# A 128-byte buffer in front of `hT` in a decoder trunk: the held operands of TensorE move off their multiples of 512 bytes

## The reference, cut to what matters

```python
def swiglu(h, w_gate, w_up, w_down):
    return (jax.nn.silu(h @ w_gate) * (h @ w_up)) @ w_down
...
for layer in range(DEPTH):
    h = rms_norm(x, mix_norm[layer])
    x = x + hybrid_mixer(h, w_in[layer], ...)
    h = rms_norm(x, ffn_norm[layer])
    if layer % 2 == 0:
        x = x + swiglu(h, dense_w_gate[i], dense_w_up[i], dense_w_down[i])
    else:
        x = x + moe_ffn(h, router_w[i], moe_w_gate[i], moe_w_up[i], moe_w_down[i])
return rms_norm(x, final_norm)
```

## Time and profile before

| | |
|---|---|
| median of 3 runs | 1428.15 us (1425.51 to 1428.62) |
| the profiled execution's own time | 1425.18 us |
| its span, first to last instruction | 1423.6 us |
| granted TensorE clock | 0.998 |
| TensorE matmuls, weight loads | 6506 each |
| HBM traffic over the span | 313 GB/s |

### The profile page before, as it was taken

The page is one execution under the profiler, slowest core; times in us unless marked ns, Lnnn a source line. Parts: engine busy times, 40 slices in busy tenths (PEclk is TensorE's granted clock), DMA queues, the critical chain, the costliest instruction groups (busy, mean ns, idle before and its releaser), DMA issues.

```text
span 1423.6 us, 18360 instructions
## 1 busy us (share of the span) xinstructions
PE 1409.4 (99%) x6506; PEld 1168.6 (82%) x6506; DVE 1174.7 (83%) x1068; ACT 986.9 (69%) x876; POOL 207.9 (15%) x249
## 2 busy tenths in 40 slices
PE   9999999999999999999999999999999999999997
PEld 7888888888888888888888888888888888888885
DVE  6987544548987998889899898888989989888896
ACT  7765444347765877867877777786787777778674
POOL 6840000005831001001001001000100100100010
PEclk9999999999999999999999999999999999999999
DMA  9656555545548899999999999999999999999990
GB/s 359 222 169 215 178 181 198 183 162 196 175 164 310 283 386 378 371 370 409 375 382 372 390 367 371 388 370 369 412 372 384 370 391 366 371 389 373 366 411 33
DMA packets 197552, 445.96 MB, mean 313 GB/s; under 512 B 8400, under 2 KB 19968, under 8 KB 197504
## 3 DMA queue, kind: packets, MB, share of 16 engines
q1 hardware_dynamic: 192496, 432.57, 80.4%
q0 software_dynamic: 2304, 8.39, 2.2%
q10 hardware_dynamic: 2704, 4.38, 0.9%
HBM read 437.97 MB, written 7.34 MB: 313 GB/s over the span
## 4 chain that ended last, share of the span: by engine, by line
issue 58%; PE 34%; POOL 4%; DVE 2%; ACT 1%; DMA 0%; POOLq 0%; ACTq 0%; DVEq 0%
PE bank L1467 10%; PE bank L1469 10%; PE bank L1468 10%; POOL small L611 2%; POOL gates L614 2%; DVE w_lo L989 1%; POOL sums L621 1%; PE bank L1528 1%; DVE bank L1038 1%; PE bank L1631 0%; PE bank L1593 0%; ACT w_hi L654 0%; PE bank L1763 0%; PE bank L1587 0%; DVE tokA L1104 0%
## 5 line engine op out<-in xcount | busy, mean ns | idle before, releaser
L989 DVE TENSOR_TENSOR w_lo<-raw,w_hi 128x2048 fp32r<-128x2048 f32 x256 | 582.9, 2292 | 134.8 <-ACT w_hi L654 134.6
L654 ACT ACTIVATE w_hi<-raw 128x2048 fp32r<-128x2048 f32 x256 | 488.6, 1913 | 200.2 <-PE bank L1469 199.8
L1467 PE MATMUL bank<-w_hi,dT_hi 128*128 128x512 f32 (+1 forms) x756 | 296.4, 392 | 0.0
L1469 PE MATMUL bank<-w_hi,dT_lo 128*128 128x512 f32 (+1 forms) x756 | 293.2, 388 | 0.0
L1468 PE MATMUL bank<-w_lo,dT_hi 128*128 128x512 f32 (+1 forms) x756 | 292.6, 387 | 0.0
L1467 PE MATMUL bank<-w_hi,cT_hi 128*128 128x512 f32 x492 | 194.3, 395 | 0.0
L1469 PE MATMUL bank<-w_hi,cT_lo 128*128 128x512 f32 x492 | 191.7, 390 | 0.0
L1468 PE MATMUL bank<-w_lo,cT_hi 128*128 128x512 f32 x492 | 191.6, 390 | 0.0
L1469 PEld LDWEIGHTS bank<-w_hi,dT_lo 128*128 128x128 f32 x756 | 142.0, 188 | 29.4
L1467 PE MATMUL bank<-w_hi,hT_hi 128*128 128x512 f32 x416 | 164.4, 395 | 1.1 <-DVE w_lo L1086 1.0
L1468 PEld LDWEIGHTS bank<-w_lo,dT_hi 128*128 128x128 f32 x756 | 142.2, 188 | 28.1
(11 more groups left out here) (256 smaller groups left out, 1865.8 us busy)
## 6 DMA issues: line engine op xcount, KB each, us to landing
raw<-in_moe_w_gate_dram SPq DMA_DIRECT2D x96, 1024.0 KB, 7.5
raw<-in_moe_w_up_dram SPq DMA_DIRECT2D x72, 1024.0 KB, 10.3
raw<-in_moe_w_down_dram SPq DMA_DIRECT2D x72, 1024.0 KB, 8.9
raw<-in_w_in_dram SPq DMA_DIRECT2D x20, 1024.0 KB, 7.1
mix<-in_moe_w_up_dram SPq DMA_DIRECT2D x16, 1024.0 KB, 8.8
gates<-in_moe_w_down_dram SPq DMA_DIRECT2D x16, 1024.0 KB, 11.3
gates<-in_moe_w_up_dram SPq DMA_DIRECT2D x16, 1024.0 KB, 8.8
work<-in_moe_w_down_dram SPq DMA_DIRECT2D x16, 1024.0 KB, 11.5
```

Source lines behind the costliest of these rows:

```text
L654: act.activation(w_hi[split_place(u, seen.item is not None)][:, 0:width], place[slot][:, 0:width], ACT.Copy).then_inc(hi_ready, 1)
L989: dve.tensor_tensor(w_lo[split][:, 0:width], place[slot][:, 0:width], w_hi[split][:, 0:width].bitcast(F32), ALU.subtract).then_inc(lo_read ...
L1467: nc.tensor.matmul(dst, a_hi, b_hi, start=start, stop=False)
L1469: return nc.tensor.matmul(dst, a_lo, b_hi, start=False, stop=stop)
```

## The change

One buffer of 128 bytes a partition (32 float32) is declared between `work` and `hT_hi`. It is never written or read.

```diff
         xs = sb("xs", [P, TB, D])
         work = sb("work", [P, TB, D])
+        sb("by_128", [P, 32])
         hT_hi = sb("hT_hi", [P, KD, S], F32R)
         hT_lo = sb("hT_lo", [P, KD, S], F32R)
```

## The result

| | before | changed |
|---|---|---|
| median of the runs | 1428.03 us (1425.51 to 1428.62, 4 runs) | 1452.74 us (1452.13 to 1454.47, 4 runs) |
| the profiled execution's own time | 1425.18 us | 1454.47 us |
| its span | 1423.6 us | 1452.9 us |

The ratio is 1.0183 (95% interval 1.017 to 1.0196): slower by 24.7 us in the medians, by 29.3 us between the two profiled executions. (The table's two medians alone give 1.0173, inside that interval.) The forecast was no change, 1405 to 1450 us.

What follows compares the result with a forecast made beforehand. The prediction took the spacing of TensorE's matmul starts as the bound. Its terms summed to 0 on the profiled 1425.18 us; against the runs' median of 1428.15 it said 1428 us, range 1405 to 1450.

Steps and rivals of the forecast that it cites:

- What bounds the kernel: TensorE's own stream of 5808 matmuls, 226.7 ns apart, bounds it; one nanosecond per start is 5.8 us.
- Instructions, the three other engines, transfers: No instruction changes; ScalarE, VectorE, GpSimd and transfers have enough waiting or spare to hide slower accesses: zero.
- rivals 3 and 4: 3: only moved streams pay, +2.9 to +9.4 us, chance 0.14; 4: landings at 128 past make transfers the bound, chance 0.03.
- The held operands: Reading held blocks beside TensorE's stream at new addresses: taken as zero, bounds -62 to +48 us.
- a fixed toll per load: Each product pays some 11 ns for reading a new held block, whatever the addresses, so the move costs zero.
- the out-of-step rows: Starts 235 ns apart after pooling products, 230 after an expert's transposes; throughout, these would add 48 or 19 us.
- Rival 2: Load and stream meet worse on TensorE's matmuls: +19 to +48 us, so 1447 to 1476; chance 0.14.
- Rival 3: Only the 864 matmuls streaming from `hT` pay, with or without transposes: +2.9 to +9.4 us, 1431 to 1438; chance 0.14.

Runs made afterwards that it cites:

- The turns of twelve: Reference computation left out, TensorE alone: units of 12 matmuls by turns at held-to-streamed distance 0 and 128; 227.9 ns at 0, 232.7 ns at 128.
- The grids: Reference computation left out, TensorE alone, held and streamed operands placed at many offsets; 512-column products took 226.7 ns at distance 0, 232.4 at 128, 234.3 at 96.

## Why the prediction was wrong

**What bounds the kernel** was right: TensorE's starts, 5808 of them, and 5.8 us for each nanosecond. The rows with 211 waits before and after bear it out.

**Instructions, the three other engines, transfers** were right at zero. With everything moved by 128 the time is 1426.53 against 1426.39 us, so a stream or a landing at 128 bytes past is worth nothing by itself, which is what rivals 3 and 4 were about.

**The held operands** is the step that failed: "I take zero", because "a fixed toll per load, whatever the addresses, fits all of these". It was put at nothing, and it cost 5.7 to 6.2 ns on each of the 4944 products that stream from `w` and 2.9 to 3.5 ns on the 864 from `hT`, once the pace was steady: 29.9 us over all starts. What the runs show in place of a fixed toll is a pace that depends on held minus streamed address modulo 256. The bounds there were sound. The steady pace became 232.4 to 232.9 ns, between the 230 and 235 read from the out-of-step rows, which gave +19 to +48 us (measured: +24.7 in the medians). Rival 2 held, and it had 0.14. The range ended at 1450, so it took in only the lower end of that rival's 1447 to 1476. The argument for zero was weak in a way that could be seen: all distances that I called "many values" were multiples of 512, hence all the same number modulo 256, and I counted them as evidence of no dependence. The sentence after it says that no row has another distance; so it was known that the sample was empty where the change goes, and still half of the chance was put on zero. The earlier trace rows was the better witness. It showed that the same operands can lose the step, so that the 226.7 ns were a state to be lost and not a sum of fixed parts.

**The Trainium skill's rule** ("TensorE: Matmul & The Clock Gate", Part 2, step 1: two independent read ports) spoke for zero, and these runs contradict it for fp32r: moving only the held block changes the stream's pace by up to 7.6 ns (234.3 at a distance of 96) with all else idle. The pace from the same page (Part 1: N/2.4 + about 2.5 ns, from which 215.8 for 512 columns is an estimate) agrees with bf16, 215.8 ns here, and is 10.9 ns short for fp32r.

**Rival 3's remark** that the streams from `hT` would pay was the wrong way round. They moved along with what is held, kept the distance 0, and lost least: 229.6 to 230.1 ns against 232.4 to 232.9. That they lost at all goes with their short units of twelve between units that are out of step. By place in the unit, the medians over the changed kernel's 72 units are 235, 233, 234, 227, 227, 231, 228, 228, 231, 227, 227 and 227 ns, and the step at the eleventh place is 226 or 227 ns in all 72; before the change every median is 227. So each unit settles anew and has got there by its end. The turns of twelve settle after three steps (227.9 in the mean); why the full kernel takes up to ten stays open.

What stays open too is the collision itself: which reads meet, if reads do, and why the step of 226.7 ns holds at 0 modulo 256. The grids show that the pace depends on the load's and the stream's addresses together; that two reads collide is my reading of it, which nothing here shows directly.

No version beats both kernels. 226.7 ns is the lowest pace at any distance tried, and the kernel before has it in 88 of its 90 long runs.

## What to carry to other kernels

With fp32r products of 512 columns, keep held and streamed operands a multiple of 256 bytes apart: 64 or 128 off costs 2.5 to 2.9% of the steady pace, and a buffer declared anywhere between them can do it. Where the two start matters less: both at 128 is as good as both at 0. And when a trace shows no dependence, but only at places that are alike in one respect (here modulo 256), it says nothing of the change that leaves them.

## What the runs showed of the hardware that was not expected

- The pace of fp32r products has steps that a run falls into. At 0 and 256 bytes the 226.7 ns came after all 8 kinds of start, at 16 and 144 after 1 of 8, at 64 and 128 after none; and at 16 and 144 one kind of start led to 226.7 ns in one kernel and to 233.3 in another.
- bf16 and plain f32 have 215.8 ns at distance 0 and at 128, the two that were tried: neither the toll nor an effect of the distance.
- At 256 columns the distance of 64 is quicker (117.8 against 120.0 ns), at 512 slower (233.4 against 226.7).
- Loads of 64 and 32 columns under a 512-column stream made it slower than full loads, at distance 0: 230.0 and 231.7 against 226.7 ns.
